# Probabilities of eight attention pairs turned by a transposing DMA instead of TensorE

## What is computed

```python
z = x @ w_in                                   # latents, q, k, v, 3 * 1024 gate logits
o_mla = attention(q, k, v, scale)              # 8 heads, causal
o_fox = attention(fq, fk, fv, scale, cumsum(log_sigmoid(f_logit)))
o_dsa = attention over the 64 keys that an index picks per query, shared k and v
# every attention: p = softmax(scores), o = einsum('bhqk,bkhd->bqhd', p, v)
proj = einsum('bsnc,ncd->bsnd', [o_mla, o_fox, o_dsa], w_branch)
merged = sum over branches of sigmoid(gate) * proj
x = layernorm(ALPHA * x + merged @ w_out)
x = layernorm(ALPHA * x + (gelu(conv(x @ w_up)) * val) @ w_down)
```

## Time and profile before

| | |
|---|---|
| median of 3 runs | 838.59 us (838.52 to 838.93) |
| the profiled execution | 839.47 us |
| its span, first to last instruction | 837.7 us |
| PE busy | 831.2 us (99%) |
| DVE busy | 606.0 us (72%) |
| ACT busy | 464.0 us (55%) |
| POOL busy | 114.3 us (14%) |
| six transposes of a pair, all pairs (L994) | 144 instructions, 20.5 us |
| values of the pairs (L1013) | 192 instructions |
| copies of the turned probabilities by DVE (L1691) | 24 instructions |

### The profile page before, as it was taken

How to read it: one execution, slowest core, us unless ns; L and a number is a source line. 1 busy time by engine, 2 the same in 40 slices (tenths; PEclk the granted TensorE clock), 3 DMA queues, 4 the chain that set the end, 5 groups by cost and what they waited for, 6 DMA issues and landing times.

```text
span 837.7 us, 15807 instructions
## 1 busy us (share of the span) xinstructions
PE 831.2 (99%) x6383; PEld 776.4 (93%) x6383; DVE 606.0 (72%) x1080; ACT 464.0 (55%) x701; POOL 114.3 (14%) x133
## 2 busy tenths in 40 slices
PE   7999999999999999999999999999999999999999
PEld 6899999999899999988889999998998999999888
DVE  5675788987886877765676568888787687777555
ACT  5675866663456655543447576756535475555430
POOL 1503920006300000000000067000080000000000
PEclk9999999999999999999999999999999999999999
DMA  9959643444578666475847694434557767764731
GB/s 301 241 136 274 195 142 111 142 152 151 164 191 238 196 190 187 158 243 175 266 121 181 115 343 127 149 125 128 151 180 202 190 189 196 201 189 151 246 119 50
DMA packets 190265, 150.98 MB, mean 180 GB/s; under 512 B 32653, under 2 KB 164337, under 8 KB 189937
## 3 DMA queue, kind: packets, MB, share of 16 engines
q1 hardware_dynamic: 181120, 143.09, 58.4%
q10 hardware_dynamic: 9072, 6.90, 3.0%
HBM read 148.63 MB, written 1.06 MB: 179 GB/s over the span
## 4 chain that ended last, share of the span: by engine, by line
PE 91%; POOL 3%; issue 1%; DVE 1%; DMA 1%; SPq 1%; ACT 1%; POOLq 0%
PE ps L678 28%; PE ps L679 27%; PE ps L680 27%; POOL merged L2062 3%; PE ps L982 3%; PE ps L994 2%; PE ps L1013 2%; DVE w_lo L1533 1%; DMA raw<-w_in 1%; ACT w_hi L1188 1%; PE ps L757 1%; PE ps L1087 1%; PE ps L944 0%; PE ps L1079 0%; SPq L640 0%
## 5 line engine op out<-in xcount | busy, mean ns | idle before, releaser
L1533 DVE TENSOR_TENSOR w_lo<-raw,w_hi 128x2048 fp32r<-128x2048 f32 (+2 forms) x140 | 302.2, 2160 | 112.1 <-ACT w_hi L1188 112.0
L678 PE MATMUL ps<-xt_hi,w_hi 128*128 128x256 f32 x1232 | 345.0, 280 | 0.0
L679 PE MATMUL ps<-xt_lo,w_hi 128*128 128x256 f32 x1232 | 340.7, 277 | 0.0
L680 PE MATMUL ps<-xt_hi,w_lo 128*128 128x256 f32 x1232 | 340.6, 276 | 0.0
L1188 ACT ACTIVATE w_hi<-raw 128x2048 fp32r<-128x2048 f32 (+3 forms) x142 | 252.9, 1785 | 80.2 <-PE ps L680 71.0
L678 PEld LDWEIGHTS ps<-xt_hi,w_hi 128*128 128x128 f32 x1232 | 231.3, 188 | 3.3 <-issue 2.0
L679 PEld LDWEIGHTS ps<-xt_lo,w_hi 128*128 128x128 f32 x1232 | 231.6, 188 | 0.0
L680 PEld LDWEIGHTS ps<-xt_hi,w_lo 128*128 128x128 f32 x1232 | 231.5, 188 | 0.0
L678 PE MATMUL ps<-w_hi,ht_hi 128*128 128x512 f32 (+1 forms) x179 | 69.1, 386 | 0.0
L680 PE MATMUL ps<-w_hi,ht_lo 128*128 128x512 f32 (+1 forms) x179 | 69.0, 386 | 0.0
L679 PE MATMUL ps<-w_lo,ht_hi 128*128 128x512 f32 (+1 forms) x179 | 69.0, 386 | 0.0
(11 more groups left out here) (258 smaller groups left out, 1288.5 us busy)
## 6 DMA issues: line engine op xcount, KB each, us to landing
raw<-ffn_w_up SPq DMA_DIRECT2D x88, 512.0 KB, 5.2
raw<-w_in SPq DMA_DIRECT2D x84, 512.0 KB, 5.9
raw<-ffn_w_down SPq DMA_DIRECT2D x32, 512.0 KB, 4.2
raw<-w_branch SPq DMA_DIRECT2D x24, 512.0 KB, 4.7
raw<-w_out SPq DMA_DIRECT2D x16, 512.0 KB, 4.7
raw<-ffn_w_down SPq DMA_DIRECT2D x24, 256.0 KB, 3.0
decay<-decay_rows ACTq DMA_DIRECT2D x2, 1024.0 KB, 8.4
ln_g<-ln_g ACTq DMA_DIRECT2D x4, 512.0 KB, 3.4
```

Of the source, the lines that this page charges most:

```text
L678: pe.matmul(dst, a_hi, b_hi, start=first, stop=False)
L679: pe.matmul(dst, a_hi, b_lo, start=False, stop=False)
L680: return pe.matmul(dst, a_lo, b_hi, start=False, stop=last)
L1533: ins = dve.tensor_tensor(low, panel_raw(l, p)[0:n, cols], panel_hi(l, p)[0:n, cols].bitcast(F32), ALU.subtract)
```

## The change

For pairs 2 to 9 (CROSSED) the six PE transposes go away, and with them their two copies out of ps. In their place: POOL copies each head's normalised probabilities, 128 x 384 fp32 seen as 128 x 768 16-bit values, into two planes, the low and the high halves (split_probs, one copy for each head). SP issues a transposing DMA for each head, 128 x 768 of 16 bits (cross_probs), placed in its stream behind the loads of panel 20 + i, and waits there for the split. POOL joins the turned planes again into turned(i) (join_probs, one copy for each head). The new tiles lie over fq_t and fk_t, so the first split of a layer also waits for the scores of pair 3.

values(l, g) of these pairs (g = 1 to 4) goes to slot 4g+7 instead of 4g+6, which puts it into the slot of a scores(), and it now stands ahead of turn_probs in a slot. It waits for probs_joined. outputs_hi and outputs_lo follow one slot later too: slot 4g+8. row_least(i+2) waits for the split of pair i where it waited for its transposes. The 48 products at the end are taken out.

```diff
+CROSSED = range(2, PAIRS - 2)
...
+        def values_slot(g):
+
+            return 4 * g + LAG_V + (3 if 2 * g in CROSSED else 2)
...
+            def cross_probs(l, i):
+
+                for a in range(2):
+                    n = crossed_before(i, a)
+                    sp.wait_ge(s_probs_split, at("probs_split", l, n + 1))
+                    if l > 0 or n >= 2:
+                        sp.wait_ge(s_probs_joined, at("probs_joined", l, n - 1))
+                    sp.dma_start_transpose(halves_crossed[:, a], prob_halves[:, a].rearrange("p u k -> p (u k)")).then_inc(s_probs_crossed[a], 16)
...
+                    if p - GATE_AT - NLO in CROSSED:
+                        cross_probs(l, p - GATE_AT - NLO)
...
+                if 2 * g in CROSSED:
+                    pe.wait_ge(s_probs_joined, at("probs_joined", l, crossed_before(2 * g + 2, 0)))
+                else:
...
-                    for i in even_slot_pair(s, LAG_T):
-                        turn_probs(l, i)
-                    for g in fourth_slot_pairs(s, LAG_V):
+                    for g in values_in(s):
...
                         values(l, g)
+                    for i in even_slot_pair(s, LAG_T):
+                        if i not in CROSSED:
+                            turn_probs(l, i)
...
-            products_behind_last()
...
+                        if i not in CROSSED:
+                            probs_odd_out(l, i)
...
-                    for g in fourth_slot_pairs(s, LAG_V + 1):
+                    for g in values_in(s - 1):
                         outputs_hi(l, g)
...
-                    dve.wait_ge(s_probs_turned, at("probs_turned", l, 2 * i - 2))
+                    if i - 2 in CROSSED:
+                        dve.wait_ge(s_probs_split, at("probs_split", l, crossed_before(i - 2, 2)))
...
-                        if i < PAIRS - 1:
+                        if i < PAIRS - 1 and i not in CROSSED:
                             probs_even_out(l, i)
...
-                    for g in fourth_slot_pairs(s, LAG_V + 1):
+                    for g in values_in(s - 1):
                         outputs_lo(l, g)
...
+            def split_probs(l, i):
+
+                if i == CROSSED.start:
+                    pool.wait_ge(s_scores_ready, at("scores_ready", l, 4))
+                for a in range(2):
+                    pool.wait_ge(s_probs_normed, at("probs_normed", l, 2 * i + a + 1))
+                    pool.tensor_copy(prob_halves[:, a], prob[:, i % 2, a, :].bitcast(U16).rearrange("p (k u) -> p u k", u=2)).then_inc(s_probs_split, 1)
+
+            def join_probs(l, i):
+
+                pool.wait_ge(s_pairs_output, at("pairs_output", l, i // 2))
+                for a in range(2):
+                    pool.wait_ge(s_probs_crossed[a], 16 * at("probs_crossed", l, i - CROSSED.start + 1))
+                    pool.tensor_copy(turned(i)[:, a, :].bitcast(U16).rearrange("p (k u) -> p u k", u=2),
+                                     halves_crossed[:, a].rearrange("p (u c) t -> p u (c t)", u=2)).then_inc(s_probs_joined, 1)
...
+                for i in CROSSED:
+                    split_probs(l, i)
+                    join_probs(l, i)
```

More of the change, by code:

```diff
@@ L22 @@
 I32 = mybir.dt.int32
+U16 = mybir.dt.uint16
 ACT = mybir.ActivationFunctionType
@@ L90 @@
 LAST_SLOT = 2 * (PAIRS - 1) + LAG_V
+CROSSED = range(2, PAIRS - 2)
+LAG_X = 5
 B_S, B_PT, B_GATE, B_O, B_QK = (0, 1), (2, 3), (4, 5), 6, 7
@@ L129 @@
     scores_ready=PAIRS, maxima_ready=SLOTS, probs_ready=SLOTS, probs_normed=SLOTS,
-    probs_turned=SLOTS, turned_even_ready=PAIRS, turned_odd_ready=PAIRS,
+    probs_turned=2 * (PAIRS - len(CROSSED)), turned_even_ready=PAIRS - len(CROSSED), turned_odd_ready=PAIRS - len(CROSSED),
+    probs_split=2 * len(CROSSED), probs_crossed=len(CROSSED), probs_joined=2 * len(CROSSED),
     pairs_output=PAIRS // 2, outputs_hi_ready=PAIRS // 2, outputs_lo_ready=PAIRS // 2,
@@ L208, in build_program @@
         s_probs_turned = sem("probs_turned")
+        s_probs_split = sem("probs_split")
+        s_probs_crossed = [sem(f"probs_crossed_{a}") for a in range(2)]
+        s_probs_joined = sem("probs_joined")
         s_turned_even_ready = sem("turned_even_ready")
@@ L335, in build_program @@
                 gated = so("gated", [P, NGATED, T])
+            with ExitStack() as over:
+                so = sized(over)
+                prob_halves = so("prob_halves", [P, 2, 2, 3 * P], U16)
             fq_t = sa("fq_t", [P, 4, T])
+            with ExitStack() as over:
+                so = sized(over)
+                halves_crossed = so("halves_crossed", [P, 2, 6, P], U16)
             fk_t = sa("fk_t", [P, 4, T])
@@ L486, in split_behind, with crossed_before, turned_no @@
             return {0: [], 1: [4], 2: [5], 3: []}.get(p, [p + 2])
+        def crossed_before(i, a):
+            return 2 * (i - CROSSED.start) + a
+        def turned_no(i):
+            return i if i < CROSSED.start else i - len(CROSSED)
+        def values_slot(g):
+            return 4 * g + LAG_V + (3 if 2 * g in CROSSED else 2)
         def even_slot_pair(s, lag):
@@ L491, in even_slot_pair, with values_in @@
             return [i] if not odd and 0 <= i < PAIRS else []
-        def fourth_slot_pairs(s, lag):
-            return [i // 2 for i in even_slot_pair(s, lag) if i % 2]
+        def values_in(s):
+            return [g for g in range(PAIRS // 2) if values_slot(g) == s]
         def spread_rows(w, a):
@@ L988, in turn_probs @@
                 if i > 0:
-                    pe.wait_ge(s_turned_even_ready, at("turned_even_ready", l, i))
-                    pe.wait_ge(s_turned_odd_ready, at("turned_odd_ready", l, i))
+                    pe.wait_ge(s_turned_even_ready, at("turned_even_ready", l, turned_no(i)))
+                    pe.wait_ge(s_turned_odd_ready, at("turned_odd_ready", l, turned_no(i)))
                 for a in range(2):
@@ L997, in values @@
             def values(l, g):
-                pe.wait_ge(s_turned_even_ready, at("turned_even_ready", l, 2 * g + 2))
-                pe.wait_ge(s_turned_odd_ready, at("turned_odd_ready", l, 2 * g + 2))
+                if 2 * g in CROSSED:
+                    pe.wait_ge(s_probs_joined, at("probs_joined", l, crossed_before(2 * g + 2, 0)))
+                else:
+                    pe.wait_ge(s_turned_even_ready, at("turned_even_ready", l, turned_no(2 * g + 1) + 1))
+                    pe.wait_ge(s_turned_odd_ready, at("turned_odd_ready", l, turned_no(2 * g + 1) + 1))
                 if g > 0:
@@ L1081, in turn_up @@
                 ins.then_inc(s_up_turned, 1)
[L1083 to L1087, removed]
             pe.wait_ge(s_const, N_CONST)
@@ L1652, in row_least @@
                 if i >= 2:
-                    dve.wait_ge(s_probs_turned, at("probs_turned", l, 2 * i - 2))
+                    if i - 2 in CROSSED:
+                        dve.wait_ge(s_probs_split, at("probs_split", l, crossed_before(i - 2, 2)))
+                    else:
+                        dve.wait_ge(s_probs_turned, at("probs_turned", l, 2 * turned_no(i - 2) + 2))
                 if i == 0:
```

9 lines of the change are left out of this document (4 added, 5 removed).

## The result

The changed kernel takes 843.21 us (median; 841.69 to 844.10), 1.0051 times the kernel before, with a 95% interval of 1.0038 to 1.0063. By the ratio it is slower by 4.3 us (3.2 to 5.3), where 833.3 us, 5.3 us faster, was forecast. The time lies in the range 828 to 850. The profiled execution is one of 844.10 us, with a span of 842.4 us where the one before had 837.7.

What follows compares the result with a forecast made beforehand. PE was taken as the bound: 11.3 us leave it, locks cost 1.6 and slot 24 costs 4.4, net -5.3 us, taking the median from 838.59 to 833.3 us. Range 828.0 to 850.0 us.

Steps and rivals of the forecast that it cites:

- The bound: PE bounds the kernel, busy 831.2 of 837.7 us; DVE is next, at 85% in the changed stage.
- (a) The transposes: The six PE transposes of each of pairs 2 to 9 leave PE: 9.7 us gained in two layers.
- slot 24: The fourth outputs enter DVE's stream ahead of the first merges: about 2.2 us lost a layer, 4.4 in two.
- (b) Values in the shared slot: Values of g = 1 to 4 share a slot with scores, saving one entry and one exit: 1.6 us in two layers.
- The tail: Removing the 48 products at the end costs nothing; the gain is at most 0.9 us.
- The chain's terms: Odd pair's normalise to values: 0.3 rest of first split, 0.9 split, 3.8 transfer, 0.9 join; sum 5.9 us.
- rival 1: The transposing DMA is slow and PE waits at all eight places: 849.1 or 869.9 us by the row taken; chance 0.29.
- The allowance: Time the chain may take before values of g = 1 to 4: 7.9, 7.6, 6.9 and 6.5 us.
- The locks: POOL and DVE block each other where copies meet DVE instructions: 0.4 us at each of four tight places, 1.6 us.
- Rival 3: POOL's locks slow DVE until it is the bound: 846 us; chance 0.08.
- The signs and the range: PE idle under 1 us before values in slots 19 and 23; no copy over 1.8 us; range 828.0 to 850.0 us.

Runs made afterwards that it cites:

- Small copies: The changed kernel with POOL's splits and joins copying 16 of 384 columns (only the first split of each layer whole): 834.03 us, ratio 0.9938.
- the copies alone: The kernel before, plus POOL's four copies a pair for pairs 2 to 9, read by nobody, without transposing DMAs: 844.12 us, ratio 1.0066.
- seven pairs, ScalarE splits: The changed kernel with only pairs 2 to 8 crossed, ScalarE making the splits, values of g = 4 in old slot 22: 832.60 us, ratio 0.9918.
- the filler: The changed kernel with 30 identity products ahead of the wait of the values of g = 4 in each layer: 842.15 us, ratio 1.0031.
- ScalarE's splits: The changed kernel with ScalarE making the 32 splits in place of POOL, outputs of g = 4 placed as in the change: 835.73 us, ratio 0.9966.

## Why the prediction was wrong, point by point

- **The bound** was read rightly, and so was who is next: DVE's 85% is what the change ran into.
- **(a) The transposes**: right. Small copies, at 832.0 us of span with 4.4 us lost at slot 24, has 837.7 + 4.4 - 832.0 = 10.1 us from turns and shared slots together. With 0.5 us for the latter, the turns brought 9.6; 9.7 was forecast. 48 transposes of probabilities are left of 144.
- **(b) Values in the shared slot**: wrong, 0.5 for 1.6 us. The step took the 0.11 us over one transpose as an entry from fp32r, with no row in which the identity stands behind fp32.
- **The tail**: right, nothing.
- **The chain's terms**: a split of 0.83 (0.9 taken) was right, and the transfer, 2.8 us to landing, better than the 3.8 taken. Landing was under 5 us, which makes rival 1 false, the transfer being the forecast's widest bound. The Trainium skill's page "VectorE: DVE Perf Modes", section "The three transpose paths", gives 1309 ns for one block. My estimate of 7.9 us took six of them one after the other, and the trace does not agree with that: six blocks of 128 x 128 land in 2.8 us. No run has one block alone. The join is some 1.1 us when free. As a sum the chain measured 6.8 us against 5.9, of which 1.9 are the join that stood behind the low-part subtraction. The sum had 0.6 us to spare at g = 4; 0.9 us more of chain use that up and no more than 0.3 beside it.
- **The allowance** is the step that failed. 6.5 us were read for g = 4 as if normalise of pair 9 moved with PE. It was 171.37 - 167.41 = 4.0 us: scores of pair 11 came 6.3 us earlier than before (176.5 to 170.2), normalise of pair 9 only 1.0 (168.42 to 167.41). These 2.5 us less are nearly all of the wait of 2.9. With small copies normalise came 6.0 us earlier and left 8.2 us: the allowance held.
- **The locks** are the term that was mis-sized, which is why the allowance failed. The sum had 1.6 us, as 0.4 us at four late meetings on the chain. Their first effect is on DVE's own stream: 18.4 us over two layers, eleven times that term, less the 8.9 us given up. The trace lists no idle time of DVE from about 113 to 174 us, so each microsecond of it makes the next normalise late. A part of it could have been counted: a normalise that met POOL took 0.54 us longer, and there were to be 8 of them a layer, 8.6 us in all. That is near the 7.9 us that normalise lost with the copies alone, and all that DVE gives up. No row showed what a join does to it.

The rule that I cited from the Trainium skill, "SBUF — State Buffer", section "SBUF: two separate sides", agrees with the trace. Row minima with both inputs in SBUF (prob and selm) went from 0.42 to 0.52 us in the mean of their wide form in the changed kernel, and those that read PSUM stayed at 0.42. Normalise, with one tensor of SBUF as input, was blocked too; whether it runs in a two-port mode, as the rule wants it then, no run shows. I had used the rule for the chain alone.

- **Rival 3** had this mechanism, at 8%, and was priced at 846 us as a DVE that bounds by itself. The copies in the kernel before gave 844.1, so its size was near; the changed kernel's 843.2 us comes by a mixture, with DVE's lateness reaching PE through the join (5.7 us), through the row minima (1.5), and by the clock.
- **The clock** had no term: a wait of 2.9 us costs 1.5 more behind it, half as much again. That holds for waits of this length here; behind the wait of 1.42 us in seven pairs, ScalarE splits, the granted clock stayed at 1.00.
- **Slot 24**: right, 2.2 us a layer forecast and measured. The merges' waits show 3.0 of the 4.4 us; no wait names the rest.
- **The signs and the range**: PE was to be idle for under 1 us in front of values in slot 23, and no copy was to take over 1.8 us; it was 2.9 us, and a join took up to 3.0. That the time still lies in the range is luck in the main: its upper part was made for half of rival 1, a slow transfer, and the transfer was fast.

The sum with the measured terms: -10.1 (turns and shared slots) + 4.4 (slot 24) + 5.7 (join) + 3.1 (lower clock) + 1.5 (row minima) = +4.6 us; the span grew by 4.7. That they add up this well is in part luck, since waits shift one another, as the filler shows.

How much of this is the splits and how much the joins is shown in part. With ScalarE's splits (outputs as in the change) the row minima are back at 10.2 us in all, and normalise is at 38.0 us, where it had 41.8 in the changed kernel and 26.3 with small copies: 11.7 of the 18.4 us stay with the joins alone. What stays open is how the meetings of the two add up, since each moves the others. A place for the joins where DVE reads PSUM wasn't tried.

## What to carry to other kernels

Work moved to an engine whose instructions block those of a nearly full one is paid twice: count its instructions against the neighbour's stream first (meetings times the block a row shows), and then move the neighbour's milestones by the result before any slack is read off. When the bound's stream gets shorter, its producers don't move with it; a slack from the old trace holds only for an engine with idle time of its own to give. In this kernel it was the last group that decided: leaving out the last odd pair and moving half of the copies to ScalarE made a loss of some 4 us a gain of 7.

## What the hardware showed that I had not expected

- A transposing DMA of 128 x 768 16-bit values from SBUF to SBUF lands in 2.8 us, with 1.23 us of SP's queue for each issue (medians of 32), although the nearest plain SBUF to SBUF row was 9.9 us.
- A GpSimd copy that starts 0.18 us behind a 2.29 us subtraction on DVE takes 3.01 us in place of 1.1, and a row minimum of DVE behind a copy 1.22 us in place of 0.42 (in the kernel with the copies alone).
- Behind 2.86 us without a product the granted clock was 0.66 and then 0.50 in steps of 2 us, and it was back at 0.99 some 4 us after PE had begun again.
- The identity product ahead of the values takes 0.20 to 0.26 us behind fp32 scores, and 0.21 behind fp32r products.
